# Prompt selection and gate sums moved into the stage of the cached keys, the token loop reordered, key pages asked for by one queue

## The chip, the cores and the metric

The kernel runs on one core of a Trainium2 chip. The metric is the device time of one execution in microseconds (us); lower is better. Engines are named as in the profile: PE is TensorE's matmuls, PEld its weight loads, DVE VectorE, ACT ScalarE, POOL GpSimd, SP the sync engine, which here only asks for transfers.

## What is computed

Two layers of a decoder trunk for 512 prompt tokens and 8 sample tokens (one each of 8 sequences with 1024 past tokens in pages of 128). A layer projects the normalised input into four branches, multiplies each branch's output by a sigmoid gate, and adds a gated feed-forward part. The part of branch A that the change moves is the choice of keys for the prompt:

```python
def dsa_block(q, iq, iw, qpos, kidx, gather_kv, topk):
    s = jnp.einsum('bthd,bld->bthl', iq, kidx)
    score = jnp.einsum('bth,bthl->btl', iw, jax.nn.relu(s))
    score = jnp.where(admissible[None], score, NEG)
    _, idx = lax.top_k(score, topk)          # 128 of up to 512 for the prompt, 256 of 1025 for a sample
    ...
    p = jax.nn.softmax(logits, axis=-1)
```

Branch B (stick-breaking) takes log-sums over all later keys; branches C and D (mLSTM, SSD) need running sums over the tokens of the gate inputs `c_f` and `d_dt`, and a running maximum: the "gate sums".

## The kernel before

Feature-major activations of 520 columns (512 prompt, 8 sample) are multiplied by weight tiles of 128x1024, each split into a leading part (`WH`, written by ACT) and a rest part (`WL`, by DVE or POOL), three matmuls for each product. Each engine's instructions stand in an order written out by hand and wait on semaphores. All tiles pass through `R`, a ring of four slots: a tile is asked for when the tile four before it has been used. `split` and `split_rest` make the parts; `project` is one projection tile, 48 matmuls.

A layer runs in these stages, with the windows of layer 1:

- **First projections** (12 tiles, `CUT`), rotary, to 1517.3 us.
- **Key stage**, 1517.3 to 1579.7: 32 tiles of cached keys (`K`, two pages of 256 KB each) against the sample queries. A page's address is read from `PT` by `page` and then asked for in `cached_keys`. Every second tile from the sixth on is asked for by ACT (`by_act`), the others by SP.
- **Second projections** (17 tiles) beside the samples' choice of keys: 32 rounds of `max` and `match_replace` on DVE (`sx_score` to `sx_sel`), to 1710.6 with a first part of the gate product.
- **Value pages**, to 1782.6: 16 groups of four pages asked for by SP into two buffers, two groups after each of the first seven transposed tiles (`TO_TM`).
- **Sums**, to 1827.1: the gate sums (`sm_v` to `sm_em`) and the sample gates. TensorE waits for them at L737 and L756.
- **Sample rows**, to 1862.4: eight broadcasts (`r_bc`) of sample rows for the state updates.
- **State loop**, to 2040.7: eight heads of branches C and D. In each, POOL masks the decays and makes the state weights (`vu_ready`), DVE multiplies, PE sums.
- **Token loop**, 2046.5 to 2249.6: four blocks of 128 queries. In block t: four index products (L877), the logits of branch B (L884), then on ACT absolute value, exponential and logarithm, on DVE four additions (`sp_done`), on POOL four masks (`sp_mask`); PE then forms the sums (L901), ACT takes the exponential, POOL masks (`a_mask`), PE multiplies by the values (L912). DVE makes the selection, 16 rounds of `max` and `match_replace` for t of 1 and more, after `sp_done`; the attention of branch A follows.
- **Merging** from 2249.6: gate logits come back from DRAM and the branches are multiplied and added; then output projection and feed-forward part.

The gate product (32 tiles, L602) is the filler. `gates` yields after each of its 512 steps of three matmuls; `fill(n)` on PE runs it up to step n, `drain(n)` on ACT copies finished halves of 8 steps to `RB`, and `follow(n)` on POOL makes rest parts. A copy of a half waits until SP has stored the same half of the gate tile before (`g_stored`, in `keep`). The tables `LAST`, `PAST_P`, `IN_TM`, `CUM`, `ROWS`, `SEL`, `DOTS`, `IN_R`, `LOOP` and `TO_T` say up to which step each stage fills.

## Time and profile before

| | us |
|---|---|
| median of 3 runs | 2830.25 (2829.61 to 2830.66) |
| the profiled execution | 2827.99 |
| its span, first to last instruction | 2826.3 |
| PE busy, mean granted clock | 2417.6 (86%), 0.90 |
| DVE, ACT, POOL busy | 1293.8, 1018.3, 300.7 |

The profiled execution took 2.3 us less than the median of the runs, and 1.7 us of its time lie outside the span. The page gives busy times; a stage can still be bound by an engine that is busy for a small share. The table of stages tells for each window its length, the busy time of every engine with the number of its instructions, the granted clock of TensorE (1.00 is 2.4 GHz, 0.50 is 1.2 GHz), and the busy share and rate of the DMA engines. The list of waits tells what ended the idle times before a group of instructions.

### The profile page before, as it was taken

To read this page: it belongs to the slowest core of one execution; us is meant where nothing else is said; L and a number is where in the kernel's file an instruction comes from. 1 tells how busy PE (TensorE), PEld (TensorE's weight loads), DVE (VectorE), ACT (ScalarE), POOL (GpSimd) and SP (SyncE) were. 2 spreads that over 40 slices of the span, in tenths; PEclk is the share of its full clock that TensorE was granted. 3 is DMA by queue.
4 is the path that set the end of the run, shared out by engine and by line. 5 is a ranking of instruction groups with operands and counts; after the bars stand their busy time and mean duration, and the time that the engine had idled before them with its cause. 6 is when DMAs were issued, how large, how long until landed. Compare 5 with 4: busy or idle time off the path is not lost. (4 is left out here: it accounts for less than half of the span.)

```text
span 2826.3 us, 41242 instructions
## 1 busy us (share of the span) xinstructions
PE 2417.6 (86%) x16296; PEld 2079.1 (74%) x16296; DVE 1293.8 (46%) x2065; ACT 1018.3 (36%) x1534; POOL 300.7 (11%) x318
## 2 busy tenths in 40 slices
PE   6879769997789889999887897699878897999996
PEld 5659557675557789999885785676756576999895
DVE  3329224222666466563342473233236665666623
ACT  3123233333334345552230223333334333555521
POOL 0003111331110000000000131112312000000000
PEclk9989875998989899999999897769989898999998
DMA  4352540222116122222315435211211251222221
GB/s 152 124 190 88 157 126 30 68 74 65 34 41 196 60 68 90 91 96 81 107 53 176 146 97 177 93 34 57 82 46 53 63 171 45 90 90 90 91 83 60
DMA packets 111827, 263.99 MB, mean 93 GB/s; under 512 B 13458, under 2 KB 47250, under 8 KB 110738
## 3 DMA queue, kind: packets, MB, share of 16 engines
q1 hardware_dynamic: 99074, 238.25, 26.6%
q10 hardware_dynamic: 12560, 23.11, 2.5%
q8 instruction: 129, 2.11, 0.3%
q14 instruction: 64, 0.52, 0.1%
HBM read 233.71 MB, written 27.59 MB: 92 GB/s over the span
## 5 line engine op out<-in xcount | busy, mean ns | idle before, releaser
L515 PE MATMUL PS<-XH,WH 128*128 128x260 f32 x2592 | 540.5, 290 | 43.9 <-DVE XL L1360 34.4
L1036 ACT ACTIVATE WH<-R 128x1024 fp32r<-128x1024 f32 x270 | 285.9, 1059 | 720.3 <-PE PS L515 566.8
L515 PE MATMUL PS<-XL,WH 128*128 128x260 f32 x2592 | 529.0, 286 | 5.3 <-issue 5.3
L515 PE MATMUL PS<-XH,WL 128*128 128x260 f32 x2592 | 528.4, 286 | 0.0
L1384 DVE TENSOR_TENSOR WL<-R,WH 128x1024 fp32r<-128x1024 f32 x176 | 215.8, 1226 | 548.5 <-ACT WH L1036 548.1
L515 PEld LDWEIGHTS PS<-XH,WH 128*128 128x128 f32 x2592 | 408.8, 193 | 52.4 <-issue 41.9
L515 PEld LDWEIGHTS PS<-XL,WH 128*128 128x128 f32 x2592 | 406.8, 192 | 5.7 <-issue 5.7
L515 PEld LDWEIGHTS PS<-XH,WL 128*128 128x128 f32 x2592 | 406.2, 192 | 0.0
L602 PE MATMUL PS<-XH,WH 128*128 128x260 f32 x1024 | 323.3, 316 | 13.9 <-ACT RB L1054 10.1
L1760 POOL TENSOR_TENSOR WL<-R,WH 128x1024 fp32r<-128x1024 f32 x94 | 224.6, 2390 | 893.2 <-ACT WH L1036 892.7
L602 PE MATMUL PS<-XL,WH 128*128 128x260 f32 x1024 | 307.8, 301 | 0.0
L602 PE MATMUL PS<-XH,WL 128*128 128x260 f32 x1024 | 306.7, 300 | 0.0
L602 PEld LDWEIGHTS PS<-XH,WH 128*128 128x128 f32 x1024 | 212.8, 208 | 38.4 <-issue 29.0
L602 PEld LDWEIGHTS PS<-XL,WH 128*128 128x128 f32 x1024 | 212.7, 208 | 0.8
L602 PEld LDWEIGHTS PS<-XH,WL 128*128 128x128 f32 x1024 | 212.1, 207 | 0.0
L515 PE MATMUL PS<-FR,WH 128*128 128x260 f32 x1024 | 188.8, 287 | 8.9 <-issue 8.9
L1054 ACT ACTIVATE RB<-PS 128x260 f32<-128x260 f32 x128 | 49.7, 388 | 322.0 <-PE PS L602 223.3
L515 PEld LDWEIGHTS PS<-FR,WH 128*128 128x128 f32 x1024 | 152.6, 193 | 9.7 <-issue 9.7
L1363 DVE SCALAR_TENSOR_TENSOR S<-S,V 128x510 f32<-128x510 f32 (+1 forms) x176 | 132.1, 751 | 44.2 <-ACT S L1327 40.8
L948 PE MATMUL PS<-F,R 128*128 128x260 f32 x512 | 119.4, 388 | 4.2 <-DVE F L1360 2.7
L948 PEld LDWEIGHTS PS<-F,R 128*128 128x128 f32 x512 | 94.1, 190 | 29.1 <-DVE F L1360 9.6
L1360 DVE TENSOR_TENSOR F<-F,PS 128x512 f32<-128x512 f32 (+1 forms) x64 | 31.2, 488 | 168.8 <-POOL S L1797 149.7
(319 smaller groups left out, 3197.1 us busy)
## 6 DMA issues: line engine op xcount, KB each, us to landing
R<-w_up SPq DMA_DIRECT2D x88, 512.0 KB, 3.3
R<-w_gate SPq DMA_DIRECT2D x64, 512.0 KB, 3.8
R<-w_proj SPq DMA_DIRECT2D x58, 512.0 KB, 3.3
R<-w_down SPq DMA_DIRECT2D x44, 512.0 KB, 3.3
R<-k_c SPq DMA_DIRECT2D x72, 256.0 KB, 3.5
GATES<-RB SPq DMA_DIRECT2D x128, 130.0 KB, 3.8
S<-GATES SPq DMA_DIRECT2D x64, 260.0 KB, 2.7
R<-k_c ACTq DMA_DIRECT2D x56, 256.0 KB, 4.0
```

Of the source, the lines that this page charges most:

```text
L515: i = mm(PS[:, bank + a, 0:HALF], p[:, w, k * 128:(k + 1) * 128], x[:, a * HALF:(a + 1) * HALF], start=first and p is WH and x is hi, stop ...
L602: i = mm(PS[:, 1 + 2 * a, 0:HALF], p[:, half(l, m), k * 128:(k + 1) * 128], x[:, k, a * HALF:(a + 1) * HALF], start=k == 0 and p is WH and ...
L948: ins = mm(PS[:, 4 + 2 * (q % 2) + a, 0:HALF], slot(l, nb)[:, 256 * br + 128 * k:256 * br + 128 * k + 128], F[:, o + k, a * HALF:(a + 1) * ...
L1036: do(A(WH[:, half(l, m), :], slot(l, SPLIT[m]), ACT.Copy), w_hi)
L1054: do(A(RB[:, HALF * a:HALF * (a + 1)], PS[:, 1 + 2 * a, 0:HALF], ACT.Copy), g_out)
L1360: do(v_.tensor_tensor(out, a, b, op), s)
L1363: do(v_.scalar_tensor_tensor(out, a, sc, b, o0, o1), s)
L1384: v_.tensor_tensor(WL[:, half(l, m), :], slot(l, SPLIT[m]), WH[:, half(l, m), :].bitcast(f32), ALU.subtract).then_inc(w_lo.sem, 1)
L1760: g_.tensor_tensor(WL[:, half(l, m), :], slot(l, SPLIT[m]), WH[:, half(l, m), :].bitcast(f32), ALU.subtract).then_inc(w_lo_p.sem, 1)
```

## The change

Three things move.

1. Into the key stage: the 16 index products of the prompt, one after each of the key tiles 1 to 16 (into banks 0 to 2 of PSUM), ACT's relus of them, and on DVE the weighted sums and the whole selection of all four blocks. It is kept as bytes in a new buffer, `UNSEL`. The gate sums go there too, with the transposes of the gate inputs before the first key tile. `by_act` returns False: SP asks for all 64 pages. The rest parts of the first two tiles after the stage are made by POOL, behind its four masks of the selection, and no longer by DVE.
2. The samples' steps in the second projections stand later (`CUT + 1`, `+2`, `+7`, `+10`; the broadcast `sx_bc` after 16 gate steps), as DVE comes to them after the selection.
3. The token loop: no index products, relus or selection; ACT takes the exponentials of branch A (`at_exp`) ahead of those of branch B; logits of branch A all stand before the sums of branch B; the last filler of a block stands behind its attention. The tables give the value pages 4 steps a tile (6 before), the sample rows 3 each (2), a head of the state loop 24 (28) and a token block 52 (32 to 46). The number of steps, 512, stays.

```diff
-BY_POOL = NPROJ + NG - CUT - 2
+BY_POOL = NPROJ + NG - CUT
-LAST, PAST_P = 16, 24
-IN_TM = [30, 36, 42, 48, 54, 60, 66, 72, 76, 80, 84, 88]
-CUM, ROWS, SEL, DOTS = 96, 104, 108, 112
-IN_R = [DOTS + 2 * (s + 1) for s in range(8)]
-LOOP = [(IN_R[-1] + 28 * v + 12, IN_R[-1] + 28 * v + 28) for v in range(8)]
-IN_T = [[10, 8, 8, 6], [10, 8, 14, 8], [10, 8, 16, 8], [10, 8, 20, 8]]
+LAST, PAST_P = 16, 32
+IN_TM = [PAST_P + 4 * (i + 1) for i in range(11)]
+SEL, DOTS = 80, 88
+IN_R = [DOTS + 3 * (s + 1) for s in range(8)]
+LOOP = [(IN_R[-1] + 24 * v + 10, IN_R[-1] + 24 * v + 24) for v in range(8)]
+IN_T = [[14, 14, 10, 14] for t in range(NT)]
...
+        UNSEL = sb("UNSEL", [128, TRI_W], mybir.dt.uint8)
...
         def by_act(u):
-            return u >= RING and u % 2 == 1
+            return False
...
+                def index_product(n):
+                    t, h = divmod(n, 4)
+                    p0, w = 64 * (h % 2), 128 * (t + 1)
+                    if n >= 3:
+                        pe.wait_ge(*ix_relu.nth(l, n - 3))
+                    finish(mm(PS[:, n % 3, 0:w], F[p0:p0 + 64, IQ + h // 2, 128 * t:128 * t + 128],
+                              F[p0:p0 + 64, IKD, 0:w], start=True, stop=True), ix_done)
...
+                    if 1 <= u <= 16:
+                        index_product(u - 1)
+                    if u == 8:
+                        pe.wait_ge(*sm_cin.nth(l, 0))
...
+                    elif u == 16:
+                        pe.wait_ge(*sm_rt.nth(l, 0))
...
+                pe.wait_ge(*ix_relu.nth(l, 15))
+                pe.wait_ge(*sm_g.nth(l, 0))
                 for c in range(CUT, NPROJ):
                     project(c)
...
                 fill(LAST)
+                pe.wait_ge(*sx_sel.nth(l, 0))
...
+                fill(PAST_P)
                 pe.wait_ge(*sa_p.nth(l, 0))
...
                     fill(TO_T[t][0])
+                    for h in range(2, 4):
+                        pe.wait_ge(*at_max.nth(l, 4 * t + h - 2))
+                        attend(h)
...
                     values(l, t, 3)
+                    fill(TO_T[t][3])
...
+                            if 1 <= k <= 16:
+                                t, h = divmod(k - 1, 4)
+                                w = 128 * (t + 1)
+                                act.wait_ge(*ix_done.nth(l, k - 1))
+                                if t:
+                                    act.wait_ge(*ix_sum.nth(l, t - 1))
+                                do(A(S[:, h, 0:w], PS[:, (k - 1) % 3, 0:w], ACT.Relu), ix_relu)
...
                         act.wait_ge(*sx_done.nth(l, 0))
+                        act.wait_ge(*ix_sum.nth(l, NT - 1))
...
+                act.wait_ge(hs_stored.sem, 16 * (l + 1))
                 for t in range(NT):
...
+                def select(t, between=lambda k: None):
+                    dve.wait_ge(*ix_mask.nth(l, t))
+                    if t == 0:
+                        ts(unselected(t), score(t), NEG / 2, None, ALU.is_le, ALU.bypass, bias_ready)
+                    else:
+                        for k in range(TOPK_P // 8):
+                            between(k)
+                            do(v_.max(M8[:, :], score(t)))
+                            do(v_.match_replace(score(t), M8[:, :], score(t), TAKEN))
+                        ts(unselected(t), score(t), TAKEN / 2, None, ALU.is_gt, ALU.bypass, bias_ready)
...
+                for t in range(NT):
+                    pool.wait_ge(*ix_sum.nth(l, t))
+                    blk = TM[:, T_CK + t, t, :]
+                    do(g_.affine_select(out=blk, in_=blk, pattern=[[-1, 128]], compare_op=ALU.is_ge, fill=NEG,
+                                        base=0, channel_multiplier=1), ix_mask)
-                for m in range(CUT + 2, NPROJ):
+                for m in range(CUT, NPROJ):
                     split_rest(l, m)
```

TensorE in the key stage, around its sixteenth tile: L657, L659 and L667 (L675, L677 and L685 after) are the products with one key tile, L658 is an index product, L701 the transposes of the gate sums. Before:

```order
405 L657 MATMUL PS<-R,QI 32x256 [waits slot3_full]
406 L659 MATMUL PS<-R,QA 32x256
407 L667 MATMUL PS<-R,QB 32x256 x2
408 L657 MATMUL PS<-R,QI 32x256 [waits slot0_full]
409 L659 MATMUL PS<-R,QA 32x256
```

And after:

```order
413 L685 MATMUL PS<-R,QB 32x256 x2
414 L658 MATMUL PS<-F 128x512 [waits index_relu_ready]
415 L675 MATMUL PS<-R,QI 32x256 [waits slot0_full]
416 L677 MATMUL PS<-R,QA 32x256
417 L680 MATMUL PS<-F,QI 32x1
418 L682 MATMUL PS<-F,QA 32x1
419 L685 MATMUL PS<-R,QB 32x256 x2
420 L658 MATMUL PS<-F 128x512 [waits index_relu_ready]
421 L701 MATMUL PS<-K,RT 96x128 [waits row_terms_ready]
422 L701 MATMUL PS<-K,RT 96x128 x3
423 L675 MATMUL PS<-R,QI 32x256 [waits slot1_full]
```

Where TensorE waited only for pages, a relu and the gate sums now stand between two key tiles.

ScalarE in the first token block of layer 0: L1254 and L1255 (L1277, L1278) are the exponential and logarithm of branch B, L1261 (L1288) its second exponential, L1270 (L1282) the exponentials of branch A. Before:

```order
405 L1255 ACT_TABLE_LOAD
406 L1255 ACTIVATE F<-F,K 128x1280 [waits act_own]
407 L1054 ACTIVATE RB<-PS 128x260 [waits gate_half0_stored,gate_first_half_done,b_log_term_ready]
408 L1261 ACT_TABLE_LOAD [waits b_log_weights_ready]
409 L1261 ACTIVATE F<-PS 128x512 [waits gate_logits_copied]
```

And after:

```order
288 L1278 ACT_TABLE_LOAD
289 L1278 ACTIVATE F<-F,K 128x1280 [waits act_own]
290 L1068 ACTIVATE RB<-PS 128x260 [waits gate_half0_stored,gate_first_half_done,b_log_term_ready]
291 L1282 ACT_TABLE_LOAD [waits a_max_ready]
292 L1282 ACTIVATE S,MX<-S,MX 128x128 [waits gate_logits_copied]
293 L1282 ACTIVATE S,MX<-S,MX 128x128 [waits a_max_ready,a_exp_ready] x3
294 L1288 ACTIVATE F<-PS 128x512 [waits b_log_weights_ready,a_exp_ready]
```

The table of the exponential is now loaded for branch A, before branch B's second exponential.

## Rows read from the trace of the kernel before

**Rows 1.** Busy time by stage, layer 0's key stage, then layer 1
```profile
core 0: us, PE busy (x) PEld busy (x) DVE busy (x) ACT busy (x) POOL busy (x), PEclk, DMA share, GB/s
118.40:184.80 66.40, 41.88 (x290) 19.05 (x290) 0.55 (x2) 1.34 (x2) 0.00 (x0) 0.81 0.77 245
...
1517.30:1579.70 62.40, 39.39 (x290) 16.56 (x290) 1.27 (x2) 2.23 (x3) 0.00 (x0) 0.86 0.80 260
1579.70:1710.60 130.90, 123.54 (x940) 117.58 (x942) 88.34 (x110) 42.19 (x55) 45.95 (x19) 0.93 0.30 98
1710.60:1782.60 72.00, 46.20 (x289) 30.30 (x288) 20.47 (x40) 21.12 (x36) 7.07 (x3) 0.74 0.63 185
1782.60:1827.10 44.50, 29.73 (x204) 28.37 (x200) 12.77 (x51) 19.41 (x33) 4.75 (x2) 0.81 0.24 74
1827.10:1862.40 35.30, 35.25 (x241) 32.04 (x241) 17.47 (x23) 1.83 (x3) 2.36 (x1) 0.50 0.02 8
1862.40:2040.70 178.30, 165.43 (x957) 123.52 (x956) 48.28 (x66) 72.61 (x107) 56.34 (x87) 0.90 0.22 65
...
2046.50:2249.60 203.10, 161.25 (x840) 115.89 (x841) 107.68 (x263) 79.77 (x148) 29.47 (x44) 0.88 0.16 49
```

**Rows 2.** Timeline of the SP queue, start us, us, what
```profile
1760.37 3.63 SPq L466 DMA_DIRECT2D S<-v_c  x4
1764.78 3.63 SPq L466 DMA_DIRECT2D TM<-v_c  x4
```

**Rows 3.** DMA issues: count, KB each, us to landing
```profile
R<-k_c SPq DMA_DIRECT2D x72, 256.0 KB, 3.5
```

**Rows 4.** Selection groups on DVE: busy us, mean ns, idle before
```profile
L1481 DVE MAX8 M<-TM 8x8 f32<-8x1025 f32 x64 | 77.9, 1217 | 22.5 <-ACT TM L1094 20.4
...
L1683 DVE MAX8 M<-HS 128x8 f32<-128x256 f32 (+2 forms) x96 | 53.9, 561 | 3.3
L1684 DVE MATCH_REPLACE8 HS<-M,HS 128x256 f32<-128x256 f32 (+2 forms) x96 | 52.0, 542 | 0.0
...
L1684 DVE MATCH_VALUE_LOAD HS<-M,HS 128x8 f32 x96 | 8.8, 92 | 3.3
```

**Rows 5.** Rest parts of weight tiles, by VectorE and by GpSimd
```profile
L1384 DVE TENSOR_TENSOR WL<-R,WH 128x1024 fp32r<-128x1024 f32 x176 | 215.8, 1226 | 548.5 <-ACT WH L1036 548.1
...
L1760 POOL TENSOR_TENSOR WL<-R,WH 128x1024 fp32r<-128x1024 f32 x94 | 224.6, 2390 | 893.2 <-ACT WH L1036 892.7
```

**Rows 6.** Waits of TensorE, whole span: us in total, times, longest
```profile
PE PS L901 <- POOL F L1754: 38.6, 8, 5.5
...
PE PS L912 <- POOL F L1754: 13.6, 8, 1.8
...
PE PS L877 <- ACT S L1250: 12.7, 8, 4.7
PE PS L737 <- DVE SMT L1360: 12.7, 2, 6.3
...
PE PS L695 <- DVE TM L1366: 10.8, 2, 5.4
PE PS L756 <- DVE SS L1360: 10.6, 2, 5.4
```

**Rows 7.** Chain, state loop of layer 1: start us, us, what
```profile
1967.23 1.07 ACT WH L1036
...
1974.79 1.08 PE PS L814 x4
...
1982.90 5.84 PE PS L602 x48
```

**Rows 8.** Chain, one pair of gate steps among the sample rows
```profile
1829.12 1.60 PE PS L602 x6
```

**Rows 9.** Chain, second token block of layer 1
```profile
2100.16 0.61 ACT F L1253
...
2109.72 2.08 PE PS L901 x2
```

**Rows 10.** Chain, last token block of layer 1
```profile
2216.22 4.09 DMA GATES<-RB
```

261 lines of the change are left out of this document (128 added, 133 removed).

## The prediction

> **What bounds the kernel now.** I read the table of stages first [rows 1], since TensorE is busy for 86% of the span and the question is where it is not. In each row the reader compares the length with PE's busy time and the granted clock. In the key stage of layer 1 PE is busy 39.4 of 62.4 us, and the DMA share is 0.80: the pages set the pace. In the second projections it waits 7.4 of 130.9 us, in the value pages 25.8 of 72.0 (transfers again, 0.63), in the sums 14.8 of 44.5, in the state loop 12.9 of 178.3 and in the token loop 41.8 of 203.1. The sample rows have no gap, but their clock is 0.50, that is 1.2 GHz. Then I read who ends PE's waits [rows 6] and, for single places, the chain [rows 7 to 10]. All of the change lies between the first projections and the merging; the rest I leave as it is, save one transfer.
>
> The stages are summed for layer 1, with T the first key matmul. The filler has 512 steps before and after, so a stage that holds fewer steps is shorter only by what another pays; all of it is in the sum. A step costs 5.84/16 = 0.365 us at full clock [rows 7] and 1.60/2 = 0.80 among the sample rows [rows 8].
>
> **Key stage, 62.4 before.** This is the place with a new cost. Two requests by one queue: on SP four requests of value pages start 4.41 us after the four before them [rows 2], 1.10 us for each, and nothing else stood between them. Before, ACT asks for 28 of the 64 pages; after, SP asks for all. The first eight requests (four slots) come before T; 56 are left, 56 x 1.10 = 61.6 us, starting near T+3.5, so the last is asked at T+65.1 and lands some 2.8 us after its start (3.5 is the median of a busier queue [rows 3]). With 0.9 us for its matmuls the pages alone give T+67.9. A tile then takes 2.2 us, against 62.4/32 = 1.95 before.
>
> The second thing in the stage is DVE's selection. Its rounds with 96 pairs of `max` and `match_replace` per two layers are 53.9 + 52.0 + 8.8 + 3.3 us idle [rows 4], so 59 us a layer (16 rounds each of 256, 384 and 512 columns, near 0.99, 1.25 and 1.52 us a round). In order: sums of block 0 at T+10, gate logarithms T+14, gate sums T+20.8, selection of 256 columns to T+37, weighted sum of block 2 to T+39.2. TensorE's index product 15 (tile 16) wants a relu that wants that sum; it would arrive at T+35.5, so it stalls about 4.4 us, of which the ring hides 3.6 and the queue of requests loses about 1.6. The pages end at T+69.5. Independently, DVE ends the third block at T+66 and its last sum at T+69: two bounds within a microsecond.
>
> The third is the first weight tile after it. Its request stands after the last pages, it lands near T+71.1, ACT needs 1.06, and its rest part is now POOL's: 2.39 us where DVE took 1.23 [rows 5]. DVE's stood ready before; now 1.06 + 2.39 is exposed. First projection at T+74.7. Bounds: 68 if neither the stall nor POOL is felt, 80 if both are felt wholly and the third selection delays POOL's mask. I take 74.7, **+12.3**; in layer 0, where the stage took 66.4 before [rows 1], **+8.3**.
>
> The Trainium skill, page "DMA: Bandwidth & Descriptors", section "Issuing engines are not separate DMA queues", speaks for this part of the change and against my term: issuing from several engines saves only the sequencer's time to start a transfer, usually small beside the transfer. By that rule the key stage would keep its 62.4 us of pages.
>
> **Second projections, 130.9, steps 24 to 32.** The samples' rounds, 32 of about 2.5 us [rows 4], start only when the prompt's selection ends (T+95.5) and end near T+190. PE's wait at L695 (5.4, now for later steps) becomes about 2.2 since the samples' steps stand later; two new waits, for `sa_p` and the transposed probabilities, 1.9 and 1. Eight steps more (+2.9), and the index products and relus of the samples move within it: **-2.4**. Queued behind the new wait on `sx_sel` are the transposed tiles. Bound: +6 if the rounds are interrupted as before and end that much later.
>
> **Value pages, 72.0, steps 36 to 28.** SP-bound: 56 x 1.10 = 61.6 [rows 2] plus the stores and gate tiles between groups. Fewer of these fall in the stage; **-4.6**. Bounds 0 and -7.
>
> **Sums, 44.5, steps 46 to 28.** 18 steps go, 18 x 0.365 = 6.6 at full clock, 8 at this stage's; both waits on DVE, 6.3 and 5.4 us (12.7 and 10.6 for two layers [rows 6]), go, because the gate sums are made 100 us earlier; the transposes and cumulative products that moved are 3.3. Together 44.5 - 7.9 - 12.4 - 3.3 = 20.9: **-23.6**. This term is the surest. What is late next there is the sample gate, about 3 us, which I keep.
>
> **Sample rows, 35.3, steps 16 to 24.** Eight steps more. The row before shows 1.2 GHz while PE has no gap [rows 1, 8]; ahead of it lay the stage with the waits (0.81). I take the same level: 8 x 0.80 = **+6.3**. If the stages ahead are dense enough that the clock stands at 2.4 GHz, it is 8 x 0.365 more on a stage of half the length; that is the better rival.
>
> **State loop, 178.3, steps 224 to 192.** 32 steps go, -11.9 with their small gaps. They were cover. A head's POOL work waits for ACT and DVE; where a gate tile ends at a head, ACT's split of the next one starts at 1967.23 and PE's next matmul of the head is released at 1974.79, 7.6 us later [rows 7]; with 1.6 for ACT to come to it I take 9.2. In other heads no tile ends there. Now tiles end exactly after heads 1, 3 and 5 (steps 160, 208, 256), and the cover until PE needs the weights is 14 steps x 0.365 = 5.2: three gaps of 4 us, smaller ones elsewhere. Gaps go from 7 to 17.6: **-1.5**. Bounds -11.9 (gaps stay) and +8 (every head shows one).
>
> **Token loop, 203.1, steps 160 to 208.** Added: 48 x 0.365 = 17.5. Gone: 16 index products, 8.4, and the waits for the relu, 12.7 over eight [rows 6], 6.3 a layer. PE's wait at the sums of branch B is the largest of all, 38.6 over eight, 4.8 each [rows 6]: from ACT's absolute value at 2100.16 to PE's release at 2109.72 are 9.6 us [rows 9]. Its cover before was gate steps; now 14 or more stand ahead (IN_T), so it falls to about 3.3 in blocks 1 to 3. In block 0 ACT waits first for the states' store, which is new; there 11. The mask wait at L912, 13.6 over eight [rows 6], goes, as ACT's branch A exponentials come earlier. In the last block ACT's copy of a half stands behind SP's store, whose transfer begins at 2216.22 [rows 10]; that gap of 5.1 us stays, and about 5.4 comes with it, because the exponentials of branch A now stand between. DVE, freed of 59 us of selection, is not late anywhere here. Sum: 203.1 + 17.5 - 8.4 - 6.3 - 5.0 - 6.8 = 194.1: **-9.0**. Bounds -18 (no second half-copy gap) and 0.
>
> **Merging.** The last gate tile ends at the end of the loop; its store and load, near 4.1 us for one gate store with its wait [rows 10], are no longer covered: first use 4.5 us later, **+4.5**.
>
> **Sum.** Layer 1: 12.3 - 2.4 - 4.6 - 23.6 + 6.3 - 1.5 - 9.0 + 4.5 = -18.0. Layer 0: 4.0 better in the key stage, whose length before was 66.4, and otherwise as here: -22.0. Together -40.0; 2828.0 - 40.0 = 2788.0. The profiled execution stands 2.3 below the median of the runs, so 2790.
>
> **Rivals.** (1) *Denser clock and covered loops.* The state loop's gaps stay at 7, 10.6 less a layer, and the sample rows run at 2.4 GHz, half of 41.6, so 20.8 less a layer; either alone gives 20 to 40 us. I put the rival at the first, or the second in one layer: 2790 - 21 = 2769. For it: the stages ahead of the rows lose 12 us of waits. Against: the rows were cold with no gap in them, and PE was busy 30 of the 44 us ahead.
> (2) *One queue asks as fast as two*, the skill's rule: the queue of requests costs nothing, the selection alone bounds the stage at T+69 and POOL's rest part still follows. 2.5 us a layer: 2785. Against: the four requests at 1.10 us [rows 2] with DMA share 0.63.
> (3) *The loops give less.* Each moved wait turns up again behind the next one (half-copies, POOL's masks), 10 us a layer: 2810. For it: PE's waits there are for chains of ACT, DVE and POOL, not for DVE's load [rows 6, 9].
> (4) *Slower: SP's queue is slower than 1.10 us a request.* It has 56 requests a layer, 112 in all, against a gain of 40 us: it decides from 1.10 + 40/112 = 1.46 us. At 1.6 us the time is 2790 + 56 = 2846. For it: each key page is 256 KB by an address read from `PT`, and the 3.5 us median [rows 3] has not been seen with SP alone. Against: value pages are read the same way at 1.10.
> (5) *The change doesn't do what it says of the queue*: the transfers themselves, not requests, pace the stage (0.80, 260 GB/s [rows 1]): then 64 pages of 256 KB, 16.8 MB, at 260 GB/s take 64.5 us, the same as my 67.9 within 3. It changes the reading, not the time.
>
> **How the numbers follow.** Forecast 0.56 at 2790 (own range 2775 to 2806: the ends of the key stage, 6 us a layer either way, and of the two loops, some 8, taken as independent, 10 a layer, of which the layers share a part); rival 1 0.16; rival 2 0.08, rival 3 0.10; rival 4 0.10. Nearly all of the first four is faster by more than 0.2% (5.7 us), about what a measurement of this kernel can tell from no change: 0.83. Within it 0.06, mostly the far end of rivals 3 and 4; slower 0.11. The range takes in rivals 1 to 3: 2764 to 2824, leaving rival 4 and the part of rival 1 in which both layers run hot.
>
> **What would show it.** In the profile after: the key stage 73 to 76 us with a request every 1.10 us on SP and a wait at L658 of 4 us near its tile 16; sums near 21 us with no wait on gate sums; sample rows at clock 0.50 and 41 us (if near 25, rival 1); three gaps of 4 us after heads 1, 3, 5; L901's wait about 22 us a layer. A key stage over 80 us or requests over 1.46 us apart would make the prediction wrong, as would PE waits in the token loop as large as before.

## The result

| | us |
|---|---|
| the kernel before, median | 2829.9 (2828.6 to 2830.7) |
| the changed kernel, median | 2811.0 (2804.9 to 2814.9) |
| forecast | 2790, range 2764 to 2824 |
| profiled execution before, after | 2827.99, 2804.94 (spans 2826.3, 2803.2) |

The ratio to the time before is 0.9930, with a 95% interval of 0.9917 to 0.9943. On another chip it was 0.9910 (0.9893 to 0.9927), with runs from 2802 to 2813. So the change is faster by 19 to 24 us, half of the 40 that were forecast. The runs of the changed kernel lie 10 us apart in the first comparison and 11 in the second; those of the kernel before lie 2 and 8.5 apart.

The stages of the two profiled executions, cut at the same TensorE instructions, with the forecast beside them:

| change in us | forecast | layer 0 | layer 1 |
|---|---|---|---|
| key stage | +8.3 / +12.3 | +10.2 | +13.8 |
| second projections | -2.4 | +1.1 | +1.2 |
| value pages | -4.6 | -3.0 | -2.9 |
| sums | -23.6 | -21.8 | -21.4 |
| sample rows | +6.3 | +6.2 | +5.2 |
| state loop | -1.5 | -0.2 | +1.3 |
| between the loops | 0 | +1.7 | +0.7 |
| token loop | -9.0 | -15.8 | -17.1 |
| merging and all behind it | +4.5 | +8.8 | +6.6 |

With +2.4 ahead of the first key stage these add up to the -23.1 of the spans, within rounding. The table of stages of the changed kernel, layer 0's key stage and then layer 1, answers to [rows 1], with the same columns:

```profile
120.83:198.16 77.33, 54.79 (x335) 21.57 (x335) 53.88 (x145) 17.09 (x31) 3.60 (x6) 0.85 0.71 218
1506.82:1583.05 76.23, 54.66 (x336) 21.20 (x335) 54.13 (x145) 17.15 (x31) 3.60 (x6) 0.84 0.73 221
1583.05:1715.10 132.05, 125.35 (x962) 119.51 (x962) 105.26 (x143) 41.95 (x58) 48.59 (x21) 0.95 0.29 94
1715.10:1784.27 69.17, 37.00 (x247) 21.32 (x248) 20.41 (x45) 18.19 (x31) 4.39 (x2) 0.78 0.62 180
1784.27:1807.32 23.05, 17.52 (x131) 16.99 (x131) 7.08 (x35) 12.44 (x21) 3.55 (x2) 0.87 0.36 115
1807.32:1847.77 40.45, 40.45 (x264) 37.25 (x265) 18.02 (x19) 2.20 (x4) 3.55 (x2) 0.50 0.07 20
1847.77:2027.41 179.64, 160.89 (x861) 114.77 (x860) 45.98 (x66) 68.93 (x101) 51.46 (x85) 0.86 0.19 56
...
2033.96:2219.93 185.97, 164.72 (x953) 127.64 (x954) 40.79 (x99) 77.72 (x139) 35.38 (x43) 0.93 0.20 59
```

The key stage has 54.7 us of TensorE's work where it had 39.4, and 41 of the 57 us of DVE's rounds; the rest, those of the fourth block, end at T+93. The rows stand at clock 0.50, as forecast. The token loop has its clock at 0.93 and not 0.88, and only 21 us without TensorE's work, where it had 42. TensorE's waits over the whole span, answering to [rows 6] (us in total, times, longest):

```profile
PE PS L918 <- POOL F L1808: 20.3, 8, 7.0
PE PS L606 <- ACT RB L1068: 15.9, 10, 5.1
PE PS L835 <- DVE F L1383: 15.8, 6, 4.1
PE PS L962 <- DVE F L1383: 11.6, 16, 4.5
PE PS L796 <- ACT S L1214: 11.1, 2, 5.5
...
PE PS L732 <- DVE TM L1389: 9.3, 2, 4.7
PE PS L832 <- DVE F L1383: 9.1, 4, 4.1
PE PS L519 <- POOL WL L1814: 8.0, 2, 4.2
...
PE PS L658 <- ACT S L1106: 7.6, 2, 4.4
```

L918 is the old L901: 20.3 us, against 38.6. In each layer they are 7 us in the first block and 1.2, 1.7 and 0.4 in the others. The waits for the gate sums are gone. New or larger are, for the two layers: the state loop (L832, L835: 24.9, where L811 and L814 had 14.6 for the same release by DVE), the merging (L962), the sample gates (L796, 5.5 before), the first rest part (L519), the wait for ACT's copy of a gate half (L606, 15.9 against 10.1), and the halt at the sixteenth index product (L658).

### The profile page after: what moved, and what is told of

It reads as the page before. It is cut to its first block, busy times and chain, and to the rows that moved or that the text cites. A ratio compares the mean times of both kernels' runs of the same rounds, so it can differ in the third digit from the quotient of the medians.

```text
span 2803.2 us, 41237 instructions
## 1 busy us (share of the span) xinstructions
PE 2428.6 (87%) x16296; PEld 2077.8 (74%) x16296; DVE 1285.2 (46%) x2061; ACT 1018.3 (36%) x1534; POOL 310.0 (11%) x322
## 4 chain that ended last, share of the span: by engine, by line
PE 64%; DVE 14%; ACT 7%; SPq 4%; issue 4%; DMA 3%; POOL 3%; ACTq 0%; DVEq 0%; POOLq 0%
PE PS L519 36%; PE PS L606 8%; PE PS L1007 3%; DVE TM L1570 2%; SPq L410 2%; DVE M L1569 2%; DVE S L1386 2%; PE PS L962 2%; PE PS L863 2%; SPq L470 1%; PE PS L897 1%; ACT WH L1050 1%; POOL WL L1814 1%; DVE F L1383 1%; POOL F L1808 1%
## 5 line engine op out<-in xcount | busy, mean ns | idle before, releaser
L519 PE MATMUL PS<-XH,WH 128*128 128x260 f32 x2592 | 536.7, 289 | 52.4 <-DVE XL L1383 36.6
L519 PE MATMUL PS<-XL,WH 128*128 128x260 f32 x2592 | 527.2, 285 | 5.6 <-issue 5.6
L519 PE MATMUL PS<-XH,WL 128*128 128x260 f32 x2592 | 525.5, 284 | 0.0
L519 PEld LDWEIGHTS PS<-XH,WH 128*128 128x128 f32 x2592 | 405.8, 191 | 61.2 <-issue 48.1
L519 PEld LDWEIGHTS PS<-XL,WH 128*128 128x128 f32 x2592 | 404.6, 191 | 6.0 <-issue 6.0
L519 PEld LDWEIGHTS PS<-XH,WL 128*128 128x128 f32 x2592 | 403.1, 190 | 0.0
L606 PE MATMUL PS<-XH,WH 128*128 128x260 f32 x1024 | 323.3, 316 | 19.7 <-ACT RB L1068 15.9
L1814 POOL TENSOR_TENSOR WL<-R,WH 128x1024 fp32r<-128x1024 f32 x98 | 232.8, 2375 | 724.8 <-ACT WH L1050 723.8
L606 PE MATMUL PS<-XL,WH 128*128 128x260 f32 x1024 | 308.5, 301 | 0.0
L606 PE MATMUL PS<-XH,WL 128*128 128x260 f32 x1024 | 307.3, 300 | 0.0
L606 PEld LDWEIGHTS PS<-XH,WH 128*128 128x128 f32 x1024 | 212.7, 208 | 42.2 <-issue 33.3
L606 PEld LDWEIGHTS PS<-XL,WH 128*128 128x128 f32 x1024 | 213.1, 208 | 0.8
L606 PEld LDWEIGHTS PS<-XH,WL 128*128 128x128 f32 x1024 | 212.8, 208 | 0.0
L519 PE MATMUL PS<-FR,WH 128*128 128x260 f32 x1024 | 191.5, 290 | 8.9 <-issue 8.9
L519 PEld LDWEIGHTS PS<-FR,WH 128*128 128x128 f32 x1024 | 155.4, 196 | 9.7 <-issue 9.7
L962 PE MATMUL PS<-F,R 128*128 128x260 f32 x512 | 122.8, 396 | 11.6 <-DVE F L1383 11.6
L962 PEld LDWEIGHTS PS<-F,R 128*128 128x128 f32 x512 | 96.7, 194 | 37.1 <-DVE F L1383 18.6
L1383 DVE TENSOR_TENSOR F<-F,PS 128x512 f32<-128x512 f32 (+1 forms) x64 | 31.2, 487 | 174.3 <-POOL S L1856 160.1
```

The costliest lines, as they stand in the source:

```text
L519: i = mm(PS[:, bank + a, 0:HALF], p[:, w, k * 128:(k + 1) * 128], x[:, a * HALF:(a + 1) * HALF], start=first and p is WH and x is hi, stop ...
L606: i = mm(PS[:, 1 + 2 * a, 0:HALF], p[:, half(l, m), k * 128:(k + 1) * 128], x[:, k, a * HALF:(a + 1) * HALF], start=k == 0 and p is WH and ...
L962: ins = mm(PS[:, 4 + 2 * (q % 2) + a, 0:HALF], slot(l, nb)[:, 256 * br + 128 * k:256 * br + 128 * k + 128], F[:, o + k, a * HALF:(a + 1) * ...
L1383: do(v_.tensor_tensor(out, a, b, op), s)
L1814: g_.tensor_tensor(WL[:, half(l, m), :], slot(l, SPLIT[m]), WH[:, half(l, m), :].bitcast(f32), ALU.subtract).then_inc(w_lo_p.sem, 1)
```

## The experiments

Line numbers are those of the changed kernel except where the kernel before is named. All ratios are to the kernel before on the same chip.

### The change once more, and what the single queue costs

The changed kernel without an edit:

> The changed kernel once more, for the spread of its runs (2804.9 to 2814.9 so far, granted clock 0.906 to 0.896) and as the measure of its variants on this chip. If the spread comes from waits that vary, stages differ between this profile and the first; if from the granted clock alone, the busy time of equal work differs and the waits are the same. Time 2805 to 2815.

Measured: median 2806.3, ratio 0.9910, runs 2802.1 to 2812.9. Its profile has every stage within 3 us of the first one's, but for the key stage of layer 1: 82.2 us, where the first had 76.2.

One part of the change alone, in the kernel before:

```diff
-            return u >= RING and u % 2 == 1
+            return False
```

> The kernel before with SP asking for all key pages, nothing else changed: this part of the change alone. Theory 1: 56 requests of 1.10 us from T+3.5, last landed at T+67.9 in both layers, against 62.4 and 66.4 before: 5.5 and 1.5, and about 1 us each for the weight tile behind them, so +8 to +9 us in all, 2838. Theory 2 (the queue costs nothing): within 2 us of before.

Measured: median 2848.2, ratio 1.0059 (1.0041 to 1.0078), so 17.7 us slower: twice the forecast. The two key stages of its profile:

```profile
119.25:192.42 73.17, 43.82 (x291) 15.47 (x291) 1.30 (x2) 2.26 (x3) 0.00 (x0) 0.80 0.75 229
1526.00:1599.97 73.97, 47.07 (x290) 16.25 (x291) 1.33 (x2) 2.30 (x3) 0.00 (x0) 0.75 0.75 228
```

73.2 and 74.0 us, where the kernel before has 67.2 and 62.4 cut this way: +6.0 and +11.6, which is the whole 17.7. The queue does what was forecast: 56 requests from T+2.7 to T+64.5 (T+64.8 in layer 0), with a median of 1.10 us between two; the forecast had the last at T+65.1. What was too small is the tail. The first weight tile is asked for behind the last page and lands at T+70.6 and T+71.4, some 2 and 3 us after that page. In the kernel before, last page and weight tile landed together, at T+64.7 and T+59.8. The expectation had set the landing of the last page (T+67.9, measured T+68.6 and T+68.1) against whole stage lengths before, which hold this tail already.

So one queue costs. The Trainium skill, page "DMA: Bandwidth & Descriptors", section "Issuing engines are not separate DMA queues", weighed in the prediction, says that several issuers save only the sequencer's time to start a transfer, usually small beside the transfer. The trace agrees that it is this time that is saved, but it is not small here: 1.10 us a request, beside 2.9 from request to landing, and of the 55 distances between two requests only 3 or 4 are over 1.3 us, the longest 1.8.

### Two queues in the changed kernel

```diff
         def by_act(u):
-            return False
+            return u >= RING and u % 2 == 1
```

> The change with ACT asking for every second tile of keys from the sixth on again; all else is that of the change. Theory 1 (SP's 1.10 us a request sets the pace, the selection is a second bound close behind): SP's last request comes some 8 us earlier, then POOL's mask of the fourth block (T+68) and its rest part (2.4) hold the first projection: it starts near T+71 where it started at T+76.2, so 5 us a layer less, 10 in all. Theory 2 (which queue asks costs nothing, the transfers set the pace): the stage keeps its 76 us, no change. Theory 3 (the selection on DVE sets the stage): no change either, but with pages landing early and ACT or POOL waiting for the last index sum.

Measured: median 2814.5, ratio 0.9948 (0.9931 to 0.9965). Not faster but 8 us slower than the change on the same chip, whose interval (0.9893 to 0.9927) it does not touch; key stages of 77.6 and 78.8 us in its profile. Theory 1 had given 71. The trace shows a cause: DVE, behind its second block, waits for a copy of ACT. In the changed kernel this is the piece (start us, us, engine and line):

```profile
1544.75 1.86 ACT L1106 ACTIVATE S<-PS 128x512 f32<-128x512 f32 x3 [10.69 <-DVE TM L1386]
...
1545.40 2.07 PE L658 MATMUL PS<-F 64*128 64x512 f32 x2 [3.29 <-ACT S L1106]
1547.40 1.09 PE L701 MATMUL PS<-K,RT 128*96 128x128 f32 x4
1547.56 0.60 ACT L1106 ACTIVATE S<-PS 128x512 f32<-128x512 f32 x1 [0.95 <-PE PS L658]
...
1548.59 0.59 ACT L1115 ACTIVATE SROW<-PS 96x512 f32<-96x512 f32 x1 [0.43 <-PE PS L701]
...
1549.28 1.22 DVE L1549 TENSOR_TENSOR_SCAN SROW<-SROW 4x512 f32<-4x512 f32 x1 [4.64 <-ACT SROW L1115]
```

DVE's sum of block 2 frees ACT's relus, one of these frees TensorE's sixteenth index product, only then come the transposes of the gate sums (L701), ACT copies them, and DVE, 4.6 us idle, scans. The prediction had the halt of TensorE but not DVE's own. In the kernel with two queues the same wait is 8.6 us:

```profile
1555.26 1.21 DVE L1549 TENSOR_TENSOR_SCAN SROW<-SROW 4x512 f32<-4x512 f32 x1 [8.60 <-ACT SROW L1115]
```

since ACT's requests (1.05 us each) and their waits for used tiles stand between its relus, and its relus hold up its requests. DVE's last index sum, that of the fourth block, then comes at T+76 and not T+68, and POOL's mask and first rest part behind it. That it is the order which holds the stage up was read from this trace; the runs with another order test it.

### Without the rounds

```diff
                         for k in range(TOPK_P // 8):
                             between(k)
-                            do(v_.max(M8[:, :], score(t)))
-                            do(v_.match_replace(score(t), M8[:, :], score(t), TAKEN))
+                            if k == 0: do(v_.max(M8[:, :], score(t)))
+                            if k == 0: do(v_.match_replace(score(t), M8[:, :], score(t), TAKEN))
```

> The change with one round of max and match_replace for a block instead of 16, so the prompt's choice of keys is not the reference's; 45 rounds a layer, near 56 us of DVE, are left out. Theory 1: the wait for the relu at tile 16 (3.3 us) goes, the requests still take 56 x 1.10, so the key stage is 2 to 3 us shorter; the wait at L732 for the samples' choice (4.6) goes: 7 us a layer, 14 in all. Theory 3 (DVE sets the stage): the stage is 6 us or more shorter by itself. If the DVE work has been free where it stands now: no change.

Measured: median 2796.9, ratio 0.9886 (0.9870 to 0.9903), 9 us less than the change, of 14 expected. Key stages 74.9 and 73.3: the stage of one queue alone. So DVE's 56 us cost 2 to 3 us a layer there, besides the cases with a low clock (below). The halt at L658 went, and the last request came at T+64.4, as with one queue in the kernel before. The wait at L732 did not go, which falsified that step: it was 4.6 us a layer again, and the second projections stayed at 132 us. DVE itself stands still ahead of it:

```profile
1636.50 0.42 DVE L1383 TENSOR_TENSOR S<-S,PS 128x256 f32<-128x256 f32 x1 [14.83 <-PE PS L724]
```

This row is of the changed kernel itself: the samples' rounds stand still for 14.8 us until TensorE makes the cumulative product after tile `CUT + 7`. Without the prompt's rounds they stand still for 15.6 to 16.0 us. So their end, and with it the wait of 4.6 us at L732, is set by where this product stands, and not by when the selection of the prompt ends.

### The selection's order

```diff
-                    if 1 <= u <= 16:
-                        index_product(u - 1)
+                    if 1 <= u <= 12 or 17 <= u <= 20:
+                        index_product(u - 1 if u <= 12 else u - 5)
...
-                    elif u == 16:
+                    elif u == 12:
                         pe.wait_ge(*sm_rt.nth(l, 0))
```

and the same places in ACT's order, its copy after tile 12.

> The change with the last four index products after the key tiles 17 to 20 instead of 13 to 16 (their relus too), and the transposes of the gate sums and their copy after tile 12 instead of 16 and 18. One queue. Theory 1b (the selection's chain: DVE's scan waits 4.6 us for a copy that waits for transposes behind an index product that waits for a relu behind DVE's own sum; TensorE's halt of 3.3 to 5.7 us at L658 takes the requests of SP with it): both waits go, the last request comes at T+65 as in the kernel before with one queue, the selection of the third block ends 4 us earlier; first projection at T+74 to T+75 in both layers (76 to 82 measured), and the wait at L732 (4.6) goes: 3 to 6 us a layer for the stage and 4 for the wait, 14 to 18 in all against the change. Theory 1 (requests alone): 2 us a layer. Theory 3 (DVE's load, not the order): no change.

Measured: median 2806.7, ratio 0.9918 (0.9887 to 0.9948): no gain that can be told from the change's. TensorE's halt and DVE's wait went, and the last index sum came at T+63.2, 4 us earlier, as expected. The wait at L732 stayed at 4.6 us in layer 1 (1.4 in layer 0). The key stage still took 78.2 and 78.9 us, now with the clock at 0.55 and 0.57 in its third quarter and the last request at T+69. Theory 1b gave 75. The same with two queues, run twice:

> As the run above, with ACT asking for every second tile of keys again. Theory 1b: ACT is no longer held by a relu while it should ask for pages, and DVE no longer waits for it, so the two queues now help: first projection at T+68 to T+71, 4 to 6 us a layer less than the run above. Rival (ACT's requests of 1.05 us each between its relus hold back the selection whatever the order): as long as the run above, or longer, with the third block's sum after T+70.

> Two queues with the moved index products once more: its profile shows 69.1 us for the key stage in both layers (78.2 and 78.9 with one queue) and ended at 2790, while its other four runs took 2801 to 2815. If the second queue's gain is real in each run, this profile shows 69 to 71 again and the median falls to 2790 to 2795; if the order in which two queues' pages land varies from run to run, the stage varies by 5 to 10 us and the median stays at 2800 to 2810.

Measured: medians 2808.7 and 2802.2 (0.9927 and 0.9911), runs from 2790 to 2815. Of the four key stages in the two profiles three took 69.1 us and one 75.8. Both profiled executions, 2790.1 and 2790.0 us, are the fastest of their kernel's runs, so the profiles show it at its best. So the second queue can give 9 us a layer when the order lets it, and something takes it away in most runs. ACT's requests between its relus are not that: the last index sum, which the rival had after T+70, came at T+66 in the stages of 69.1 us and at T+68 in the one of 75.8.

### What makes the key stage long: the clock

The profiles of the versions with the selection in the key stage show one pattern: every stage of 82 us or more has a mean granted clock of 0.77 or less, and every stage of 69 us one of 0.82 or more. Between these it is loose (73.3 us at 0.80, 78.2 at 0.87). Two quarters of a stage, first of the run with SP's earlier stores (below), then of the second run with the moved order:

```profile
1494.17:1583.62 89.45, 73.18 (x336) 26.49 (x335) 55.01 (x147) 17.53 (x33) 3.60 (x6) 0.63 0.63 188
1516.53:1538.89 22.36, 22.36 (x71) 7.66 (x71) 18.39 (x58) 2.64 (x6) 0.59 (x2) 0.50 0.52 142
```

```profile
1502.09:1571.14 69.05, 50.30 (x335) 20.78 (x335) 48.88 (x135) 18.66 (x35) 4.42 (x6) 0.90 0.75 244
1519.35:1536.62 17.27, 15.20 (x112) 6.90 (x114) 13.55 (x44) 3.32 (x7) 0.29 (x1) 1.00 0.85 273
```

In the first, at 1.2 GHz, TensorE is busy for all of 22.36 us and makes 71 matmuls; in the second, at 2.4 GHz, 112 in 17.27 us. The transfers fall to 0.52 in the first: they wait for slots, since SP's pairs of requests, one pair a tile, come 3.1 to 3.9 us apart there and not 2.2. A tile of keys takes TensorE 1.93 us at the low clock and 1.06 at the high one, an index product of 512 columns 2.07 and 1.12. A tile alone stays below the 2.2 us of one queue at either clock, and just below the 1.95 of two. With such a product behind it, it needs 4.0 us at the low clock and 2.2 at the high one: TensorE becomes the bound where the clock is low. To test it, all products were made 128 columns wide:

```diff
-                    finish(mm(PS[:, n % 3, 0:w], F[p0:p0 + 64, IQ + h // 2, 128 * t:128 * t + 128],
-                              F[p0:p0 + 64, IKD, 0:w], start=True, stop=True), ix_done)
+                    finish(mm(PS[:, n % 3, 0:128], F[p0:p0 + 64, IQ + h // 2, 128 * t:128 * t + 128],
+                              F[p0:p0 + 64, IKD, 0:128], start=True, stop=True), ix_done)
```

with ACT reading these 128 columns several times, so that its and DVE's work stays. First in the changed kernel:

> The change with each index product 128 columns wide instead of 128 to 512 (the choice of keys is then not the reference's); ACT's and DVE's work, the waits and the requests are as before. In twelve profiles the key stage took 69 to 89 us and was longer the lower the granted clock in it: at 1.2 GHz TensorE itself was busy throughout its second quarter. Theory 4 (at the low clock the index products make TensorE the bound, and whether the clock is low there differs from run to run): with 3072 of 5120 columns gone it is not the bound at either clock; the stage takes 73 to 77 us in both layers, the median falls by 4 to 10 us against the change on the same chip, and the slowest run by more than the fastest. Rival (the spread comes from the transfers, the clock follows it): the stage still takes over 80 us in some layer and the spread of the runs stays above 10 us.

Measured: median 2801.1, ratio 0.9908 (0.9891 to 0.9925), stages 77.1 and 77.7. The stages are as expected: at a clock of 0.76 one takes 77.7 us with narrow products, where the changed kernel itself took 82.2 at 0.77. But the gain of 4 to 10 us did not come: the median is not clear of the change's (0.9910). So in the changed kernel the wide products at a low clock cost no time that the runs can tell; one queue and the halt (4.2 and 4.6 us here) hold the stage near 77 us in any case. It was repeated where both are gone, on the fastest version (its edits come below), beside that version itself:

> The fastest version once more, as the measure of the next run: 2707 to 2718, key stages of 69 us where the clock stays high after the first quarter, and 76 to 84 where it falls to 1.2 GHz.

> The fastest version with each index product 128 columns wide (the choice of keys is then not the reference's). Here nothing else holds the key stage near 77 us. Theory 4 (index products at the low clock make TensorE the bound): both stages take 67 to 71 us whatever the clock, the median falls by 5 to 12 us against the run beside it and the spread shrinks. Rival (the transfers vary and the clock follows): at least one stage over 75 us, and the same spread and median.

Measured: 2721.2 (2715.8 to 2730.6) with the full products, ratio 0.9612, 3 us above what was expected; 2698.9 (2697.1 to 2702.1) with the narrow ones, ratio 0.9532 (0.9519 to 0.9545). The key stages, full and then narrow:

```profile
119.66:203.76 84.10, 66.18 (x335) 25.81 (x335) 59.33 (x157) 17.49 (x33) 4.43 (x6) 0.70 0.62 196
1468.80:1544.85 76.05, 60.31 (x335) 23.13 (x335) 55.62 (x148) 17.49 (x33) 4.44 (x6) 0.77 0.68 216
```

```profile
120.82:190.28 69.46, 50.09 (x335) 22.42 (x335) 48.89 (x135) 18.25 (x33) 4.42 (x6) 0.82 0.76 243
1454.42:1523.38 68.96, 47.09 (x335) 22.27 (x335) 48.90 (x135) 16.21 (x30) 4.38 (x5) 0.87 0.77 244
```

84.1 and 76.1 us against 69.5 and 69.0. Behind the first key stage no other stage of the two profiles differs by more than 0.7 us, and the start is 1.2 longer in the second. The spread of the runs fell from 15 to 5 us. This is theory 4, and the rival (transfers that vary) is out: they had the same requests, and nothing was taken from them. The wide products cost this time at the low clock only, for the same program, with wide products, had this key stage of layer 1 in its first execution, on another chip:

```profile
1460.29:1529.12 68.83, 49.84 (x335) 20.84 (x335) 48.89 (x135) 19.06 (x35) 4.43 (x6) 0.90 0.75 245
```

68.8 us at 0.90, and 76.1 at 0.77: one program, two executions. What makes the clock differ between them, the chip or something else, stays open. The narrow stages had 0.82 and 0.87, so none of them shows what a clock of 0.70 would cost there.

### The fill points of the state loop

```diff
-LOOP = [(IN_R[-1] + 24 * v + 10, IN_R[-1] + 24 * v + 24) for v in range(8)]
+LOOP = [(112 + 24 * v + 14, min(112 + 24 * v + 28, 304)) for v in range(8)]
```

> The change with the state loop's fill points 4 steps later (first head 28 steps, last head 20; the same 192 in all), so that no gate tile ends where a head's steps end. Theory: the gaps of 3 to 4 us at L832 and L835 before heads 3, 5 and 7 are the chain behind a gate tile's end; they go, 10 us a layer, 20 in all. Rival: the wait is for the state weights (POOL and DVE), whatever tile ends there: the gaps stay or move to other heads, no change.

Measured: median 2783.8, ratio 0.9828 (0.9802 to 0.9854): 48 us less than before, where the change has 19 to 24. The loop of layer 1 took 165.9 us and not 179.6:

```profile
1842.65:2008.56 165.91, 150.67 (x862) 111.93 (x861) 45.98 (x66) 68.89 (x101) 51.33 (x85) 0.91 0.21 61
```

The waits for DVE at L832 and L835 fell from 24.9 to 5.8 us, those for ACT's copy of a half (L606) rose from 15.9 to 28.1, and the clock from 0.86 to 0.91. The rival is out: it was the tile's end that met the head's. But only 3.5 of the 13.7 us are idle time of TensorE; its busy time for the same work fell by 10.2, from 160.9 to 150.7, at the higher clock. That the gaps had held the clock down is likely and was not shown by itself.

### No steps in the sample rows

```diff
-IN_R = [DOTS + 3 * (s + 1) for s in range(8)]
-LOOP = [(IN_R[-1] + 24 * v + 10, IN_R[-1] + 24 * v + 24) for v in range(8)]
+IN_R = [DOTS for s in range(8)]
+LOOP = [(IN_R[-1] + 27 * v + 12, IN_R[-1] + 27 * v + 27) for v in range(8)]
```

> The change with no gate steps among the sample rows; a head of the state loop fills 27 steps instead of 24. Theory: the clock stands at 1.2 GHz in the sample rows because of what the rows themselves are, and a step costs 0.80 there and 0.365 in the loop: the stage goes from 40.4 to 21 us, the loop gains 24 x 0.365 = 9 less the gaps that the longer heads cover and the ends of tiles that no longer meet the ends of heads: 10 to 18 us a layer less. Rival: the clock is low because of the wait at L796 before and would follow into the loop when the rows are short: then the loop's first heads cost up to 6 us more a layer.

Measured: median 2750.3, ratio 0.9717 (0.9696 to 0.9738), 82 us less than before, so some 57 less than the change: far more than the 20 to 36 expected, since the edit also takes the ends of tiles off the ends of heads. Rows and loop of layer 1:

```profile
1776.64:1799.51 22.87, 21.03 (x192) 20.65 (x193) 16.79 (x19) 5.47 (x7) 1.19 (x1) 0.50 0.00 1
1799.51:1968.96 169.45, 158.73 (x932) 120.62 (x932) 44.28 (x66) 65.67 (x98) 53.01 (x86) 0.92 0.22 64
```

The rows are 17.6 us shorter: the 24 steps cost 0.73 each there. 16 of these steps stood among the rows in the kernel before too; the change had added 8. The rows stay at 0.50 by themselves. The loop, with 24 more steps, is 10 us shorter than the change's. The rival's cost did not come: the clock rises 16 us into the loop, where it rose 19 us into the change's.

### SP's stores of the last gate tiles

```diff
                 for d in range(2):
-                    tile(l, AT["br", d], w_br[l, d], 1024)
-                for q in range(NG - RING, NG):
+                    tile(l, AT["br", d], w_br[l, d], 1024); keep(NG - RING + d)
+                for q in range(NG - RING + 2, NG):
                     keep(q)
```

> The change with SP's stores of gate tiles 28 and 29 asked for before the request of the second merging tile, which waits for gate tile 29 to be used. Theory: ACT's copy of half 58 waits 5 us in the last token block only because SP stands at that request; the wait goes, 5 us a layer, 10 in all, less 2 a layer where POOL's mask is late next (L929). Rival: the copy waits for the transfer of the store itself (4 us): no change.

Measured: median 2796.8, ratio 0.9864 (0.9827 to 0.9901). By the medians, each against its kernel before, that is 7 to 12 us less than the change; the interval overlaps that of the change's second comparison (0.9893 to 0.9927), so the times alone do not settle it. Layer 1's key stage in the profile was the one of 89.4 us. The token loop:

```profile
2035.21:2209.49 174.28, 160.32 (x952) 124.43 (x953) 40.78 (x99) 77.86 (x139) 35.40 (x43) 0.95 0.22 63
```

174.3 us against 186.0: 11.7 less a layer, of which the merging takes 1.3 back. It is more than the 5 of the wait: POOL's mask behind it (L929, 2.4) is no longer late either, and the busy time fell by 4.4 at a clock of 0.95 and not 0.93. The wait was never for the transfer, but for SP's place in its queue.

### Together

> The change with all that helped, and more: moved index products, two queues, no gate steps in the sample rows, 16 more steps before the rows (under the wait of 5.5 us at L796), the state loop's ends 4 or 8 steps off the tiles' ends, the samples' cumulative product one projection earlier (the 4.6 us at L732 should go, since DVE stood 14.8 us waiting for it), the last gate steps of the token loop before the last attention, and SP's earlier stores. From the 2750 of the bare rows: key stage -16, L796 -8, L732 -9, last block and merging -14, loop about 0: 2700 to 2715. If the waits only move, above 2730.

> The same with one queue: if one queue costs 9 us a layer in the key stage as the two profiles say, 15 to 20 us more than the run above; if nothing, the same.

Measured: 2729.1 (0.9634) and 2731.1 (0.9642), 14 us and more above the 2700 to 2715 expected of the first. The stages from the sums to the state loop took 224 us, where the run with bare rows had 215. The edit changed two things there, and no run parts them: the stages ahead of the loop became 3 us longer with the 16 steps more, and the loop, with 16 fewer and other fill points, 5.6 longer (175.1, at clock 0.89, against 169.5 at 0.92). The second projections fell from 132.1 to 126.5, and the wait at L732 went in every version with the cumulative product one tile earlier. With two queues the key stages were 83.6 and 78.8 (clock 0.72 in both), with one 73.6 and 79.2 (0.85 and 0.76): at a low clock the second queue gives nothing. Without the 16 steps, and then also without the early last steps:

> As the run above, and the last gate steps of the token loop before the last attention: the merging starts 4 to 8 us sooner a layer (its first gate tile comes back earlier), but ACT and TensorE wait more within the loop. If the two cancel as the sum of both stages in the earlier runs says, the same as the run above within 5 us.

> The change with the moved index products, two queues, bare sample rows, 27 steps a head, the samples' cumulative product one projection earlier and SP's earlier stores; not the 16 steps under the wait at L796, and not the earlier last steps of the token loop. In the run with these two, the stages from the sums to the state loop took 224 us a layer against 215 with the bare rows alone, and the last two stages were equal. So 9 us a layer less than its 2729: 2705 to 2715.

Measured: 2711.5 (0.9592, 0.9572 to 0.9612) with the last steps early, 2719.1 (0.9602, 0.9581 to 0.9623) without, 4 above what was expected. The first has the lowest median here, 4.1% below the kernel before; but its second comparison gave 0.9612 (0.9593 to 0.9630), so it is not clear of the other. In the profile with the early last steps the merging and all behind it took 575.4 us in layer 1, against 585.0 without: the forecast's mechanism for the merging was right, and its cover in the token loop costs about as much (183.4 against 174.4). The second projections with the cumulative product one tile earlier, the same profile:

```profile
1529.12:1655.72 126.60, 123.23 (x963) 118.90 (x963) 108.58 (x153) 40.49 (x54) 49.56 (x21) 0.96 0.32 101
```

## Why the prediction was wrong

It had the sign, and its range held the time, but the gain was half of the 40 us forecast. By stages, what was lost against the forecast is 17 us in the profiled execution: 32 in the other stages and the start, less 15 that the token loop gave on top. Seven of the nine terms came out less favourable than forecast. The largest shortfalls, for both layers, are the second projections (7.1 us), the merging (6.4), the state loop (4.1), the sums (4.0) and the key stage (3.4); another 4.8 us stand at the start and between the loops, where the forecast had nothing. That the range held is luck: the 15 us of the token loop came by a term that does not follow from the forecast's own figures (below), and without them the median would be near 2826, outside it (an estimate, 2811 + 15).

**Second projections: the step that failed.** The forecast said that TensorE's wait at L695 "becomes about 2.2 since the samples' steps stand later", and took 2.4 us off the stage. It took DVE's load for what decides. It is the place of the cumulative product: DVE, 14.8 us idle, stands waiting for it. The wait was 4.6 us and the stage grew by 1.2. With 56 us of DVE's rounds left out the wait was 4.6 again; with the product one tile earlier it went, and the stage took 126.6 us and not 132.1.

**Key stage: right in kind, mis-sized, and one engine left out.** The stage took 77.3 and 76.2 us, forecast 74.7 for both. The halt at the sixteenth index product was forecast at 4.4 us and was 4.4 and 3.3 (5.7 at most in the second profile). But the loss of the queue of requests was put at 1.6 us and was 3 to 4: the last request came at T+69.0 and T+67.6, where one queue alone ends at T+64.8 and T+64.5. DVE's own wait of 4.6 us for the copy behind that product was overlooked: the step "TensorE's index product 15 (tile 16) wants a relu that wants that sum" was not followed on to who waits behind TensorE. Besides, the forecast left TensorE out of the stage, since it was busy for 39 of 62 us. The added index products make 54.7 of it, and at the low clock they make TensorE the bound. This fits the stage of 82.2 us (clock 0.77) in another execution of the same kernel, which is over the 80 us that the forecast had named as a sign of being wrong, and the 76 to 89 of its near variants. It is not what halved the gain: in the changed kernel itself narrow products bring no time that the runs can tell (0.9908 against 0.9910).

**One queue: right.** The 1.10 us a request and the end of the requests were right to 0.6 us, and in the changed kernel the first weight tile landed 4.2 and 4.5 us after its request, as taken (4.4, from T+66.7 to T+71.1); it was 5.4 and 6.5 in the kernel before with one queue. By itself the move costs 17.7 us; in the changed kernel undoing it gains nothing (2814.5), as long as the order stands as it does.

**Value pages and sums: right in kind.** -3.0 and -21.6 for -4.6 and -23.6. What was late next in the sums was the sample gate, as said, but at 5.5 us and not 3. The forecast took 12.4 us for two waits that it gives as 6.3 and 5.4, which is 0.7 too much.

**Sample rows: right.** 40.45 us at clock 0.50, forecast 41.6. What the forecast accepted as given, that steps among the rows cost 0.80 each, is what the experiment shows as the largest single loss; a third of these steps, 8 of 24, are the change's own.

**State loop: right in mechanism.** Gaps of 4.0, 4.0 and 3.0 us after the heads that were named. The term was 1 to 3 us too favourable.

**Token loop: in favour, and by luck.** The forecast expects waits of 11 us in block 0 and 3.3 in the others at the sums of branch B, 20.9 a layer, which is 1.6 more than the 19.3 before; yet its sum takes 5.0 off for them, and leaves out the 5.4 that it says comes with the gap in the last block. By its own figures the term would be -2.4 or +3.0 and not -9.0. Measured are 10.2 a layer (7.0, 1.2, 1.7 and 0.4). The chain is as long as before (ACT starts at 2085.36, TensorE at 2094.93: 9.6 us again, [rows 9]). It is better covered: besides the 14 steps, the second pair of branch A's logits (L905) now stands in front of it. The idle time fell from 41.8 to 21.3 us, and the busy time rose by 3.5 only, where the steps less the index products make 9.1 at full clock: the stage stood at 0.93 and not 0.88. The gap of 5 us in the last block stayed, as said, and SP's place in the queue is its cause.

**Merging: right in mechanism, mis-sized.** 4.5 us at its head as forecast (L962), but 6.6 to 8.8 in all: the first loads and a stretch at a lower clock behind them. With the cover put back it took 575.4 us in layer 1, 576.7 in the kernel before.

## What to carry to other kernels

A stage that is bound by transfers can take other work only as far as every engine stays below its bound at the low clock too: add the moved work at its 1.2 GHz durations, not at the mean of the profile. When small steps fill waits, ask where they run: a step in a stage that stands at the low clock costs twice (0.73 us against 0.365), and a tile's end that meets a group's end exposes a whole chain. When an engine waits for a chain, follow the chain on to what else is queued behind that engine. The wait at L732 and the one in the last token block were decided by the place of one product and of one store, and not by an engine's load; the halt at L658 went both when the load was taken off DVE and when the product was moved.

## What the runs showed of the hardware

- The granted clock of the key stage differs between the layers and the executions of one program: 0.74 and 0.90 in the two layers of one, 0.70 and 0.77 in those of another on another chip, with stages of 76.8, 68.8, 84.1 and 76.1 us. Over the versions with full products it lies between 0.63 and 0.90. In the version where TensorE is near the bound, narrow products took 22 us of 2721 away. The Trainium skill ("TensorE: Matmul & The Clock Gate", Part 1) says of a kernel's start that how many matmuls run at the low clock varies from run to run, and calls the cost below 1% of a typical kernel. Here the variation is in the middle of a kernel, at 0.8%; no run here measures the start by itself.
- The sample rows run at 1.2 GHz in the changed kernel and in the one with bare rows, where TensorE is busy for 21.03 of 22.87 us. In the two versions with 16 more steps ahead of them, where TensorE does not wait 5.5 us for the sample gate, the rows begin at 2.4 GHz and the clock falls to 1.2 after 3.2 to 4.3 us, though TensorE waits for nothing longer than 0.3 us; it rises again 14 to 17 us into the state loop. Which property of these small matmuls (8 rows by 64 or 128 columns) brings it down was not tried.
- The first 512 KB weight tile behind the stream of key pages landed 3.3 to 7.7 us after its request, over all profiles; the median over a whole profile is 3.3.
